# Expert loop of a hybrid decoder layer: 32x32 block transposes and a shuffle on VectorE in place of TensorE flips and bias matmuls

## The reference, cut to what matters

```python
logits = h @ router_w + router_b                    # 512 tokens x 32 experts
top_v, top_i = lax.top_k(logits, 4); gates = softmax(top_v)
# for every expert e, its tokens in blocks:
gu = xblk @ w_gate_up[e] + b_gate_up[e]             # 1024 -> 2048
gate, up = min(gu[:, :1024], 7), clip(gu[:, 1024:], -7, 7)
act = (up + 1.0) * (gate * sigmoid(1.702 * gate))
y = act @ w_down[e] + b_down[e]                     # 1024 -> 1024
out[token] += y * gate_of_token
```

## Time and profile before

| | us |
|---|---|
| median of three runs | 1429.55 (1427.65 to 1431.92) |
| the profiled execution | 1427.33 |
| its span | 1425.6 |
| TensorE busy | 1286.2 (90%) |
| VectorE busy | 496.2 (35%) |
| ScalarE busy | 324.7 (23%) |
| GpSimd busy | 299.4 (21%) |
| DMA, mean rate over the span | 319 GB/s |

### The profile page before, as it was taken

One profiled execution on the slowest core, in us unless ns is written; L12 is line 12 of the kernel. 1 busy time (PEld: TensorE's weight loads), 2 busy tenths in 40 slices (PEclk: granted clock), 3 DMA queues, 4 the chain that ended last, 5 costly groups with the idle time before them and its releaser, 6 DMA issues.

```text
span 1425.6 us, 33985 instructions
## 1 busy us (share of the span) xinstructions
PE 1286.2 (90%) x12484; PEld 560.1 (39%) x12485; DVE 496.2 (35%) x1476; ACT 324.7 (23%) x649; POOL 299.4 (21%) x348
## 2 busy tenths in 40 slices
PE   6999999959998999999999999888999899988870
PEld 3764544543333434444444333333443333433320
DVE  2002222443334333333333344342334333343337
ACT  2023332221312222222222222221223222222211
POOL 0513332011212212222212112130212212111210
PEclk9999999969999999999999999999999999999995
DMA  9512110224999999999989999998999989999967
GB/s 379 208 59 74 60 74 1 104 83 173 415 386 415 394 413 395 368 365 366 366 366 365 392 418 416 417 416 352 366 367 417 413 362 414 393 417 416 417 248 294
DMA packets 90869, 454.86 MB, mean 319 GB/s; under 512 B 14049, under 2 KB 14489, under 8 KB 55774
## 3 DMA queue, kind: packets, MB, share of 16 engines
q1 hardware_dynamic: 77902, 430.86, 74.5%
q0 software_dynamic: 12512, 22.11, 4.3%
q10 hardware_dynamic: 432, 1.57, 0.3%
HBM read 444.23 MB, written 14.71 MB: 322 GB/s over the span
## 4 chain that ended last, share of the span: by engine, by line
PE 73%; DMA 21%; DVE 3%; issue 1%; ACT 1%; POOL 0%; SPq 0%; DVEq 0%; POOLq 0%
PE bank L661 35%; DMA arena<-in_w_gate_up 20%; PE bank L687 14%; PE bank L421 7%; PE bank L491 4%; PE bank L437 3%; PE bank L648 2%; PE bank L626 2%; PE bank L706 1%; PE bank L450 1%; DVE xs L1284 1%; PE bank L478 1%; PE bank L464 1%; PE bank L707 1%; PE bank L616 1%
## 5 line engine op out<-in xcount | busy, mean ns | idle before, releaser
L661 PE MATMUL bank<-arena,hT 128*32 128x512 f32 x5120 | 583.9, 606 | 30.2 <-DMA arena<-in_w_gate_up 27.9
L687 PE MATMUL bank<-arena,hT 128*32 128x256 f32 x5120 | 308.4, 386 | 33.1 <-ACT hT L859 33.1
L661 PEld LDWEIGHTS bank<-arena,hT 128*32 128x32 f32 x5120 | 157.3, 111 | 393.0 <-issue 341.1
L1241 DVE TENSOR_TENSOR arena<-bank,gain 128x512 f32<-128x512 f32 x128 | 88.4, 691 | 402.0 <-PE bank L661 402.0
L687 PEld LDWEIGHTS bank<-arena,hT 128*32 128x32 f32 x5120 | 159.6, 111 | 161.3 <-issue 77.3
L963 POOL DMA_DIRECT2D ahead<-in_consts x98 | 51.6, 530 | 641.1 <-DVE hT L1260 615.3
L876 ACT ACTIVATE arena<-arena 128x256 f32<-128x256 f32 x128 | 53.3, 417 | 560.1 <-DVE arena L1243 558.7
L1260 DVE TENSOR_TENSOR hT<-bank,gain 128x256 f32<-128x256 f32 x128 | 51.4, 422 | 212.2 <-PE bank L687 206.1
L980 POOL DMA_INDIRECT y_rows<-hT,arena x80 | 82.4, 1029 | 158.3 <-DVE hT L1260 150.7
L421 PE MATMUL bank<-hT,arena 128*128 128x512 f32 x224 | 103.6, 610 | 0.8 <-ACT hT L764 0.8
L966 POOL DMA_INDIRECT hT<-h_rows,arena x82 | 84.8, 1035 | 67.9 <-issue 34.0
(11 more groups left out here) (146 smaller groups left out, 857.9 us busy)
## 6 DMA issues: line engine op xcount, KB each, us to landing
arena<-in_w_gate_up SPq DMA_DIRECT2D x256, 1024.0 KB, 6.6
arena<-in_w_down SPq DMA_DIRECT2D x128, 1024.0 KB, 15.3
arena<-in_w_in SPq DMA_DIRECT2D x10, 1024.0 KB, 18.1
arena<-y_rows SPq DMA_DIRECT2D x8, 1024.0 KB, 12.3
arena<-in_w_out SPq DMA_DIRECT2D x4, 1024.0 KB, 22.0
arena<-bias_by_dist POOLq DMA_DIRECT2D x6, 512.0 KB, 4.0
xs<-in_x SPq DMA_DIRECT2D x4, 512.0 KB, 7.4
h_rows<-arena POOLq DMA_DIRECT2D x4, 512.0 KB, 2.9
```

The lines of the kernel that those rows point to most:

```text
L661: mm = pe.matmul(bank[c][j * CH:(j + 1) * CH, :].rearrange("p (g n) -> p g n", g=2), xT[:, c, (k % 2) * P + (k // 2) * CH:(k % 2) * P + (k ...
L687: mm = pe.matmul(bank[c][j * CH:(j + 1) * CH, 0:Q], aT[:, c, (k % 2) * P + (k // 2) * CH:(k % 2) * P + (k // 2 + 1) * CH], w[:, j * Q:(j + ...
L1241: dve.tensor_tensor(gu[:, b, :], bank[c][:, :], bt[:, 0:2 * Q], ALU.add).then_inc(gu_read, 1)
```

## The change

In words. The contraction rows of a unit are taken in another order, so that a transpose of 32x32 blocks suffices to bring tokens and activations into place: unit k of `w_gate_up` now holds rows 256 j + 32 k + i in partition 32 j + i, and unit u of `w_down` the rows 256 j + 64 u + 2 i and the one behind it. `load_unit` loads them with one transfer each, as before, from a source written `j i n`. DVE transposes each chunk of `xg` and of the activations in blocks (`dve.transpose`), straight into `xT` and `aT`; the flips on TensorE, the copies on ACT and the banks between them go. The biases: ACT loads the four quarter rows of the next job's expert to partitions 0, 32, 64 and 96 of `bias_row`, and DVE spreads them to the 32 partitions of each quarter with a shuffle, in place of two matmuls and two copies. The job table gets two rows, the chunks before a job and the row transfers to be waited for, and every engine counts its semaphores by them: absent chunks are left out on all engines, under branches, with at least two chunks a job; the signal transfers go.

The diff, cut to the load, the engines' loops and what they call:

```diff
 
-            def wait_read(job, u):
+            def wait_read(job, u, low):
 
                 if u == KT - 1:
-                    sp.wait_ge(gu_done, job * NCH + NCH)
+                    sp.wait_ge(gu_done, low + AHEAD)
                 elif u == JOB_UNITS - 1:
-                    sp.wait_ge(dn_done, job * NCH + NCH)
+                    sp.wait_ge(dn_done, low + AHEAD)
                 else:
                     sp.wait_ge(units_used, job * FREED + (u + 1 - (u >= KT)))
             def load_unit(e, u):
                 if u < KT:
-                    src = w_gate_up[bass.ds(e, 1), u * P:(u + 1) * P, :].rearrange("e p n -> p (e n)")
-                    dst = ring[:, u, :]
+                    src = w_gate_up[bass.ds(e, 1)].rearrange("e (j k i) n -> (e k) j i n", j=4, i=CH)[u]
                 else:
-                    a = (u - KT) * 2 * P
-                    src = w_down[bass.ds(e, 1), a:a + 2 * P, :].rearrange("e (k p) n -> p (e k) n", p=P)
-                    dst = ring[:, u, :].rearrange("p (k n) -> p k n", k=2)
+                    src = w_down[bass.ds(e, 1)].rearrange("e (j u i k) n -> (e u) j i (k n)", j=4, k=2, i=CH)[u - KT]
+                dst = ring[:, u, :]
                 sp.dma_start(dst, src).then_inc(unit_full[u], 16)
 
-            def load_job(e, job):
...
-            def flip_x(job, a):
-
-                for c in (2 * a, 2 * a + 1):
-                    pe.wait_ge(gathered[c], job * 16 + 16)
-                for c in range(2):
-                    for h in range(2):
-                        mm = pe.transpose(bank[6 + a][:, c * Q + h * P:c * Q + (h + 1) * P],
-                                          xg[:, 2 * a + c, h * P:(h + 1) * P], ident)
-                mm.then_inc(x_tr, 1)
-
...
-                def gate(c, ks, absent=0, unflipped=0, flip=None):
+            def run_job(job, chunks, before_job, low):
+
+                def gate(c, ks):
 
                     if 0 in ks:
-                        pe.wait_ge(y_done, job * NCH + (ORDER.index(c) + 2))
+                        pe.wait_ge(y_done, before_job + (AHEAD - 1 if c else AHEAD))
                     for k in ks:
                         if c > 0:
                             pe.wait_ge(unit_full[k], job * 16 + 16)
                         w = ring[:, k, :].rearrange("p (g n) -> p g n", g=2)
                         for j in range(4):
                             mm = pe.matmul(bank[c][j * CH:(j + 1) * CH, :].rearrange("p (g n) -> p g n", g=2),
-                                           xT[:, c, (k % 2) * P + (k // 2) * CH:(k % 2) * P + (k // 2 + 1) * CH],
-                                           w[:, :, j * Q:(j + 1) * Q], start=(k == 0), stop=(k == KT - 1),
-                                           tile_position=(0, j * CH))
-                            if k == 0 and j == 0 and absent:
-                                mm.then_inc(gu_done, absent)
-                            if k == 0 and j == 1 and unflipped:
-                                mm.then_inc(t_done, unflipped)
+                                           xT[:, c, k * CH:(k + 1) * CH], w[:, :, j * Q:(j + 1) * Q],
+                                           start=(k == 0), stop=(k == KT - 1), tile_position=(0, j * CH))
                         if k == KT - 1:
...
-                def down(c, ks, absent=0):
-
-                    n = ORDER.index(c)
-                    if 0 in ks:
-                        pe.wait_ge(t_copied, job * NCH + (n + 2))
+
+                def down(c, ks):
+
+                    pe.wait_ge(act_done, low + (AHEAD - c))
                     for k in ks:
                         u = KT + k // 2
                         if c > 0 and k % 2 == 0:
                             pe.wait_ge(unit_full[u], job * 16 + 16)
                         w = ring[:, u, (k % 2) * D:(k % 2 + 1) * D]
                         for j in range(4):
-                            mm = pe.matmul(bank[c][j * CH:(j + 1) * CH, 0:Q],
-                                           aT[:, c, (k % 2) * P + (k // 2) * CH:(k % 2) * P + (k // 2 + 1) * CH],
+                            mm = pe.matmul(bank[c][j * CH:(j + 1) * CH, 0:Q], aT[:, c, k * CH:(k + 1) * CH],
                                            w[:, j * Q:(j + 1) * Q], start=(k == 0), stop=(k == KT - 1),
                                            tile_position=(0, j * CH))
-                            if k == 0 and j == 0 and absent:
-                                mm.then_inc(dn_done, absent)
                         if k == KT - 1:
                             mm.then_inc(dn_done, 1)
                         elif c == 0 and k % 2 == 1:
                             mm.then_inc(units_used, 1)
-                        if c == 1 and k == 3:
-                            flip_act(0)
-                        if c == 1 and k == 6:
-                            flip_x(job + 1, 0)
-                        if c == 0 and k == 3:
-                            flip_x(job + 1, 1)
...
-                pe.wait_ge(t_copied, job * NCH + 1)
-                pe.wait_ge(pick_done, job + 1)
-                pe.matmul(bank[4][:, 0:2 * Q], pick, bias_all[:, 0:2 * Q], start=True, stop=True).then_inc(bias_mm, 1)
-                pe.matmul(bank[5][:, 0:Q], pick, bias_all[:, 2 * Q:3 * Q], start=True, stop=True).then_inc(bias_mm, 1)
-                pe.wait_ge(x_copied, job * 2 + 2)
+
+                every = range(KT)
                 indices(job + 1)
-
-                every, rest = range(KT), range(1, KT)
+                pe.wait_ge(x_done, job + 1)
                 with pe.If(chunks > 2):
                     with pe.If(chunks > 3):
                         gate(3, every)
-                        gate(2, every, flip=3)
-                    with pe.Else():
-                        gate(2, every, absent=1, unflipped=1)
-                    gate(1, every, flip=2)
-                with pe.Else():
-                    gate(1, every, absent=2, unflipped=2)
-                gate(0, every, flip=1)
-
...
+                run_job(job, pe.value_load(jobs_i[0:1, 2, bass.ds(job, 1)], min_val=LEAST, max_val=NCH),
+                        pe.value_load(jobs_i[0:1, 3, bass.ds(job, 1)], min_val=2, max_val=COUNT_MAX),
+                        pe.value_load(jobs_i[0:1, 3, bass.ds(job + 1, 1)], min_val=4, max_val=COUNT_MAX))
 
 
         @block.scalar
         def _(act):
-            act.sem_inc(t_copied, 1)
+            act.sem_inc(sig_done, 2 + AHEAD)
...
+            def load_bias(e):
+
+                act.dma_start(bias_row[0:P:CH, :], biases[bass.ds(e * 4, 4), :])\
+                    .then_inc(bias_in, 16)
+
+            act.wait_ge(bias_zero, 1)
+            load_bias(0)
...
-                act.activation(bt[:, 0:2 * Q], bank[4][:, 0:2 * Q], ACT.Copy).then_inc(bias_copied, 1)
-                act.wait_ge(y_done, job * NCH + (NCH + 1))
-                act.wait_ge(bias_mm, job * 2 + 2)
...
+                e = act.value_load(jobs_i[0:1, 0, bass.ds(job + 1, 1)], min_val=0, max_val=E - 1)
+                chunks = act.value_load(jobs_i[0:1, 2, bass.ds(job, 1)], min_val=LEAST, max_val=NCH)
+                low = act.value_load(jobs_i[0:1, 3, bass.ds(job + 1, 1)], min_val=4, max_val=COUNT_MAX)
+
+                def sigmoid(c):
...
-                    if n >= 1:
-                        copy_act(job, n - 1)
-                copy_act(job, NCH - 1)
-                copy_x(job + 1, 0)
-                copy_x(job + 1, 1)
-
-
-            act.wait_ge(dn_done, all_down)
+
+                act.wait_ge(bias_spread, job + 1)
+                load_bias(e)
+                with act.If(chunks > 2):
+                    with act.If(chunks > 3):
+                        sigmoid(3)
+                    sigmoid(2)
+                sigmoid(1)
+                sigmoid(0)
...
             with pool.Fori(0, njobs) as job:
-                chunks = pool.value_load(jobs_i[0:1, 2, bass.ds(job, 1)], min_val=1, max_val=NCH)
-                next_chunks = pool.value_load(jobs_i[0:1, 2, bass.ds(job + 1, 1)], min_val=1, max_val=NCH)
+                chunks = pool.value_load(jobs_i[0:1, 2, bass.ds(job, 1)], min_val=LEAST, max_val=NCH)
+                next_chunks = pool.value_load(jobs_i[0:1, 2, bass.ds(job + 1, 1)], min_val=LEAST, max_val=NCH)
+                low = pool.value_load(jobs_i[0:1, 3, bass.ds(job + 1, 1)], min_val=4, max_val=COUNT_MAX)
+
+                def scatter(c):
+                    pool.wait_ge(y_done, low + (AHEAD - c))
+                    pool.sem_inc(waited_pool, 1)
+                    pool.indirect_dma_start(y_rows, bass.IndirectOffsetOnAxis(ap=idx_s[:, c:c + 1], axis=0),
+                                            yb[:, c, :], None, bounds_check=last_row, oob_is_err=False)\
+                        .then_inc(scattered, 16)
+
                 pool.wait_ge(idx_done, job + 2)
-                pool.wait_ge(x_tr, job * 2 + 2)
+                pool.wait_ge(x_done, job + 1)
                 pool.sem_inc(waited_pool, 1)
-                gather(next_chunks)
```

(87 more changed lines are left out.)

176 lines of the change are left out of this document (74 added, 102 removed).

## The result

| | before | after |
|---|---|---|
| median of four runs, us | 1428.60 (1427.46 to 1431.92) | 4116.34 (4111.94 to 4119.22) |
| the profiled execution | 1427.33 | 4119.22 |
| its span | 1425.6 | 4117.4 |
| TensorE busy | 1286.2 (90%) | 1537.0 (37%) |
| DMA, mean rate over the span | 319 GB/s | 110 GB/s |

The ratio after to before is 2.886, with an interval of 2.879 to 2.893. The forecast was 4182.

A forecast was written before the change was run, and what follows sets the result against it. Before: PE bounds three-chunk jobs, transfers two-chunk ones; after: loads on four engines. 340.4 (start) + 3750.7 (units) + 40.6 (GpSimd) + 10 (last landing) + 39.1 (tail) + 1.7 (around the span) = 4182 us; range 3950 to 4620.

The forecast's parts named there:

- four engines for a transfer: Weight loads: a source with 4 blocks outermost gets 4 engines, 104 GB/s, 10.1 us a unit instead of 2.5; chance 0.82.
- Start of the second job's loads: SP's load queue: released where the first job's last gate pass begins to free units, unchanged at 340.36 us.
- 31 jobs of transfers: Expert loop: 372 units, 390.1 MB at 104 GB/s, 3751 us, plus 41 us for GpSimd's transfers.
- After the last landing: End of the last job: landing some 2 us, then 80 down matmuls at 4.3 or 8.6 us; 10 us together.
- The tail: From the last bias addition to the end of the span: unchanged at 39.1 us.
- Additional packets for a load: SP's queue: some 4 additional packets for each weight load instead of 16.
- The chain: Profile after: the chain nearly all DMA, on `w_gate_up` and `w_down`.
- the granted clock: Profile after: the granted clock near its lower level, as PE will be mostly idle.
- The table loads: ACT: with its copies go the two table loads of 1.28 us a job.
- C: Rival, weight loads: four engines, each slower at 22.3 GB/s, 4811 us in all; chance 0.03.
- A: Rival: loads stay on 16 engines, flips' time gained, turn 3.1 us, pairs gain about 2 to 3; 1390 us; chance 0.09.
- B: Rival: as A, but PE's turn between jobs costs 4.6 us and more, giving back the flips' gain; 1427 us; chance 0.06.

## Why the prediction was right, and where it was off

**Which mechanism.** It was the forecast one, four engines for a transfer. The queue's packets show it to the unit: 56,766, of which 54,594 are rows (49,152 of weights and 5442 others), 636 belong to the 41 other transfers (41 x 16 - 20), and 1536 = 384 x 4 remain. The count of 20 that was missing before, from 33 rows on 11 engines and 1 row on one, had told what 4 blocks would do. The source's form alone makes the whole time, and 8 blocks make twice the rate.

**The sum, term by term.**
- Start of the second job's loads: forecast 340.4, measured 340.12 in SP's timeline.
- 31 jobs of transfers: forecast 3750.7 + 40.6 = 3791.3. The last unit landed at 4071.93, so it was 3731.8, and this is the miss of 59.5. It has two parts. One unit takes 9.85 us instead of 10.08: 26.6 GB/s for an engine instead of the 26.0 that I took from a stretch of before with all 16 engines busy. That is 372 x 9.85 = 3664, 87 less. GpSimd's transfers in that stretch don't explain the difference: where GpSimd is idle in it, from 1271 to 1283, the 16 engines move 413 GB/s, 25.8 each. An engine moves a little more when only four work; why was not tested. What lies beside the units is 3731.8 - 3664 = 68 instead of 40.6, 2.2 a job. In the job shown, 1.06 of it is the longer gap to 1103.86, behind three gathers at 1089 to 1093; that the rest is GpSimd's transfers too is read from the order of things, not measured. The two parts have opposite signs, so that the sum came within 2% is in part luck.
- After the last landing: forecast 10, measured 6.4.
- The tail: forecast 39.1, measured 4117.4 - 4078.31 = 39.1. Around the span 1.8.

These sum to 340.1 + 3731.8 + 6.4 + 39.1 + 1.8 = 4119.2, the profiled execution. The chain's end in after:

```profile
4029.51 42.42 DMA arena<-in_w_down
4071.93 0.04 issue
4071.97 6.32 PE bank L656 x80
4078.31 0.43 DVE hT L1201
```

**What I said the profile would show.** DMA share 2 to 3 tenths: so it was. Rate 104 GB/s: 109 to 110. Job period 121: 120.2. Landing several times 6.6 us: the page of after gives no median for these loads, and the last one took 42.42. Additional packets for a load: 4. Two were wrong. The chain is SPq 67% and DMA 18%, not nearly all DMA: the instructions on SP that issue loads are themselves held. The view of that line before, and then after (ns: shortest, median, longest):

```profile
L343 SPq DMA_DIRECT2D arena<-in_w_gate_up x256: 327/333/1035, 62.7 to 1342.9; - x128
```

```profile
L346 SPq DMA_DIRECT2D arena<-in_w_gate_up x256: 521/9141/16582, 62.3 to 3988.9; - x128
```

An issue takes 9.1 us instead of 0.33, which is near the time of one unit (9.85): with 42 us of transfers in flight, about four units, SP gets to place the next when one has been worked off. Work is limited by the same four engines either way; the chain only names the place where one waits. And the granted clock stands at 0.60 in the stretch, between its lower level (0.5 of full) and full, since the passes after each job's last unit run at a higher one: 0.86 from 1033 to 1050, after 0.50 in the 23 us before.

**The other parts.** Transposes were taken at 0.30 to 0.43 us and measured 0.411 and 0.445; the shuffle at 0.9 to 1.3 and 1.007. The table loads did not go: 48 of 1.28 us remain, where before had 32 at L869 and 32 more. That is one in each of 32 jobs and one more in each of 16 with a third chunk; it fits one load behind each branch, which is my reading of the count. They cost nothing here, behind such loads.

**The rivals.** C (slower engines) is out with 26.6. A and B can't be read in after, but their condition can be met: plain loads give 1408.8, between A's 1390 and B's 1427. A's turn was too dear (3.1 for 2.0). Its gain of 2 to 3 us a pair did not come: the pairs got longer. They were also counted wrong: of the 16 three-chunk jobs one is the first and eight follow another, so seven pairs are left and not some twelve, and A's own sum would be near 1400. Its condition was put too weakly as well: "16 engines" isn't enough. Two ways to get 16 engines gave 2023 and 2139.

## What to carry to other kernels

Before an edit rewrites the source or destination of a DMA, compare the outermost counts of both sides: four blocks against 128 partitions cost a factor of 3.6 in rate here (394 to 109 GB/s) at equal bytes and longer rows, and the queue's packet count in the profile told the number of engines for every form tried. A share of 1.0 is no full speed either: look at the GB/s beside it. Of the forms tried, one plain transfer over all 128 partitions was the fastest, and even and odd partitions in two came near it. If a layout wants rows in another order, move the permutation to where it is cheap (here four DVE instructions for a tile and host-laid small weights), and leave the large loads as they are.

## What was not expected of the hardware

- With all 16 DMA engines busy, loads moved 231 to 251 GB/s in six kernels (quarters in two, halves, 16 blocks at three distances) and 392 to 397 in three (128 rows adjacent or 64 KB apart, even and odd partitions). The busy share was 1.01 to 1.03 in the slow ones and 0.96 to 0.98 in the fast ones.
- An instruction of SP that issues a load lasts 9.1 us with about four units in flight, against 0.33 us before.
- Two queues with four-engine transfers shared one set of four (a share of 0.25 with both in flight). Splitting the loads between them cost 569 us; for part of a job the same share moved 92 GB/s instead of 106.
- Where saved TensorE time became waiting for loads, the granted clock of a pair of jobs was 0.90 instead of 1.00, and the matmuls behind the wait took 2.2 us longer than at full clock.
